# Six of a tile's 32 threshold-search passes counted on ScalarE, the final scaling on GpSimd, and the last search spread over 20 slots

## The chip, the cores and the metric

The kernel runs on one core of a Trainium2 chip. The metric is device time in microseconds (us) of one launch. Engines are called TensorE (PE in the views, PEld for its weight loads), VectorE (DVE), ScalarE (ACT), GpSimd (POOL) and SyncE (SP, which issues the loads and stores).

## The reference, cut to what matters

One inference step of a hybrid attention layer over 2048 prompt positions and 32 sample positions. The change is in the attention over the prompt. There are 8 dense heads (group A) and 8 sparse heads (group B); for B an indexer scores each pair of query and key, and each query keeps its 256 best admissible keys:

```python
rel = jax.nn.relu(jnp.einsum('bqhd,bsd->bqhs', iqb, ik).astype(jnp.float32))
score = jnp.einsum('bqh,bqhs->bqs', iwb.astype(jnp.float32) * w_scale, rel)
adm = (qp[:, None] // CHUNK) >= k_chunk[None, :]
score = jnp.where(adm[None], score, -jnp.inf)
top_val, top_idx = lax.top_k(score, topk)      # topk = 256
...
s = jnp.einsum('bqjgd,bqnjd->bqjgn', qg, kg).astype(jnp.float32) * (dh ** -0.5)
s = jnp.where(valid[:, :, None, None, :], s, -jnp.inf)
p = jax.nn.softmax(s, axis=-1).astype(v.dtype)
o = jnp.einsum('bqjgn,bqnjd->bqjgd', p, vg)
```

Around it stand the input projections before, and the output projection, a gated feed-forward layer and the norms behind.

## The kernel before

The program runs in stages with a barrier between them; `attend_prompt` is the one that changes. It takes the queries in 16 tiles of 128 (n = 0 to 15); tile n sees W = 128(n+1) keys. A tile is 16 **slots**, one for each head (h = 0 to 7 are group A, 8 to 15 group B). Each engine has its own list of instructions written out slot by slot, and semaphores that count events join them.

In slot s (tile n, head h) the engines do this:

- TensorE (block from L1843 on): the scores of the *next* head, in chunks of up to 1024 keys into the two buffers `p_s` (`product`, one chunk for W up to 1024, else two); the value products of the last head's last units; then it turns this head's probabilities over by transposes in units of 512 keys (`turn`), and for tiles with more than two units (n from 8 on) it does this in two pairs of units. Between them stand the products of the indexer for tile n+2 (`index_unit`), in slots 2 to 14.
- ScalarE: a small copy of the last head's sums (`take_halves`), the copies of the turned units out of PSUM (`take`, L1970), the ReLU of the index products (`relu`, L1977), the second pair's copies, and last the exponentials of the next head (`exps`, L1961), which wait for all of that head's minima.
- VectorE: the minimum over each chunk of the next head's scores with the mask added (`minimum`, L2098; the scaled scores go to `prob`), and then its share of the **search** for the tile n+1.
- GpSimd: for each index unit a multiply (L2049) and an add (L2055) into `score`.

The search (`search`, L2105 on) finds each query's 256th best score bit by bit: one pass for the sign and 31 passes for bits 30 to 0. A pass compares all W scores with a candidate and counts (L2118), and two instructions on one column (L2119, L2121) set the next candidate; each waits for the one before (`step`). Five more wide steps (`choose`) make the mask `chosen`, which group B's minima read. `share_by_size` deals these 37 items by an estimated size over 16 slots, from slot 2 of tile m-1 to slot 1 of tile m. The sums of a group of 8 heads are inverted and the output of 128x512 multiplied with them on VectorE in `normed` (L2159 to L2168), in slots 1 and 9.

## Time and profile before

| | us |
|---|---|
| median of 3 runs | 4330.38 (4324.39 to 4334.98) |
| the profiled execution | 4336.22 |
| its span | 4334.2 |
| busy in it: PE, DVE, ACT, POOL | 3780.9, 2278.0, 1687.5, 1350.3 |
| mean granted TensorE clock | 0.935 of full |

Shares over the whole span say little here, since the stages have different limits. The prompt attention runs from about 736 us to 2280.7 us. The stores of its outputs give the borders of its tiles: the second store of tile n-1 is issued in slot 1 of tile n, and from one such store to the next is what is called "tile n" below.

How rows are read: in the windows view a row is one stretch, from:to and its length, then the busy time with the number of instructions of PE, PEld, DVE, ACT and POOL, the granted clock of TensorE as a share of full speed, the share of DMA engines busy and GB/s. In the grouped view a row has line, engine, operation, output<-input, shape and count, then busy us, mean ns of one, and the idle time before the group's instructions. In the view in order of time a row has start, duration, engine, line, operation and shape; a bracket gives idle time just before it and what ended it. READ_ACCUMULATOR rows are the reading out of a sum.

### The profile page before, as it was taken

How to read it: one execution, taken by the hardware profiler on the slowest of the kernel's cores; microseconds unless marked ns; L12 is line 12 of the kernel's file. 1: busy time of each engine (PE TensorE's matmuls, PEld its weight loads, DVE VectorE, ACT ScalarE, POOL GpSimd, SP SyncE). 2: the span in 40 equal slices, each digit the busy share in tenths (PEclk: the TensorE clock that was granted, in tenths of full speed). 3: DMA queues.
4: the chain of work that ended last, by engine and by line, in shares of the span. 5: the costliest groups of instructions: out<-in, count | busy, mean ns of one | idle time of the engine just before them, and what ended most of it. 6: DMA issues, size and time to landing. Idle time of an engine off the chain costs nothing. (4 is left out here: it accounts for less than half of the span.)

```text
span 4334.2 us, 59271 instructions
## 1 busy us (share of the span) xinstructions
PE 3780.9 (87%) x20612; PEld 2891.5 (67%) x20612; DVE 2278.0 (53%) x4226; ACT 1687.5 (39%) x3163; POOL 1350.3 (31%) x845
## 2 busy tenths in 40 slices
PE   7999977878878888888894689699999999999998
PEld 5777743556555555565562567588878778879986
DVE  3222223799999999999943433244044224404421
ACT  3333323555556666665461222232133223213321
POOL 0000001555555556554001000134444444433332
PEclk9999988788999999999896599899999999999999
DMA  4222222110100000000001055533343433433331
GB/s 166 72 83 85 72 68 57 40 32 25 29 22 19 19 17 10 19 17 11 12 6 47 3 189 182 179 97 115 127 116 93 145 121 91 131 111 116 87 101 60
DMA packets 347844, 324.13 MB, mean 75 GB/s; under 512 B 53088, under 2 KB 285120, under 8 KB 347648
## 3 DMA queue, kind: packets, MB, share of 16 engines
q1 hardware_dynamic: 335520, 277.64, 21.9%
q10 hardware_dynamic: 7344, 26.74, 1.5%
q0 software_dynamic: 4800, 17.43, 1.0%
q8 instruction: 102, 1.67, 0.2%
q14 instruction: 78, 0.64, 0.0%
HBM read 251.57 MB, written 71.43 MB: 75 GB/s over the span
## 5 line engine op out<-in xcount | busy, mean ns | idle before, releaser
L1494 POOL TENSOR_TENSOR ff_w_lo<-ff_stage,ff_w_hi 128x2048 fp32r<-128x2048 f32 (+1 forms) x136 | 609.6, 4482 | 1212.3 <-ACT ff_w_hi L1576 1212.3
L2118 DVE TENSOR_SCALAR_CACHE_REDUCE at_hit<-at_score,at_su 128x384 bf16<-128x384 f32 (+13 forms) x434 | 641.2, 1477 | 8.6
L95 PE MATMUL ff_bank<-ff_h_hi,ff_w_hi 128*128 128x512 f32 (+1 forms) x1760 | 618.4, 351 | 30.2 <-DMA ff_h_lo<-scr_h2T 26.5
L96 PE MATMUL ff_bank<-ff_h_lo,ff_w_hi 128*128 128x512 f32 (+1 forms) x1760 | 620.1, 352 | 0.0
L97 PE MATMUL ff_bank<-ff_h_hi,ff_w_lo 128*128 128x512 f32 (+1 forms) x1760 | 618.6, 351 | 0.0
L1638 DVE TENSOR_TENSOR ff_a_lo<-ff_prod,ff_a_hi 128x512 f32 (+1 forms) x110 | 410.4, 3731 | 170.7 <-ACT ff_a_hi L1590 170.7
L1886 PE MATMUL at_p_t<-at_ident,at_prob 128*128 128x128 f32 x2176 | 346.4, 297 | 100.5 <-ACT at_prob L1961 99.0
L1576 ACT ACTIVATE ff_w_hi<-ff_stage 128x2048 fp32r<-128x2048 f32 (+1 forms) x136 | 252.9, 1860 | 443.5 <-PE ff_bank L97 416.2
L1970 ACT ACTIVATE at_probt<-at_p_t 128x512 f32<-128x512 f32 (+3 forms) x640 | 314.9, 532 | 256.3 <-PE at_p_t L1886 254.3
L1961 ACT ACTIVATE at_prob<-at_prob,at_st 128x1024 f32<-128x1024 f32 (+7 forms) x384 | 342.5, 894 | 171.1 <-DVE at_st L2098 170.7
L95 PEld LDWEIGHTS ff_bank<-ff_h_hi,ff_w_hi 128*128 128x128 f32 x1760 | 331.0, 188 | 79.9 <-issue 31.8
L2049 POOL TENSOR_TENSOR at_rel<-at_rel,at_iws 128x512 f32<-128x512 f32 (+3 forms) x304 | 285.6, 939 | 306.3 <-ACT at_rel L1977 305.8
L1886 PEld LDWEIGHTS at_p_t<-at_ident,at_prob 128*128 128x128 f32 x2176 | 249.3, 148 | 183.6 <-ACT at_prob L1961 142.8
L96 PEld LDWEIGHTS ff_bank<-ff_h_lo,ff_w_hi 128*128 128x128 f32 x1760 | 330.8, 188 | 47.2
L97 PEld LDWEIGHTS ff_bank<-ff_h_hi,ff_w_lo 128*128 128x128 f32 x1760 | 330.7, 188 | 46.4
L1873 PE MATMUL at_p_s<-kv_KA,at_qa 96*128 96x512 f32 (+3 forms) x640 | 299.6, 586 | 46.5 <-DVE at_st L2098 40.1
L2055 POOL TENSOR_TENSOR at_score<-at_rel,at_score 128x512 f32<-128x512 f32 (+3 forms) x266 | 305.0, 1147 | 20.8
L1586 ACT ACTIVATE ff_prod<-ff_bank 128x512 f32<-128x512 f32 (+1 forms) x110 | 57.0, 518 | 642.1 <-PE ff_bank L97 642.0
L95 PE MATMUL ff_bank<-ff_w_hi,ff_a_hi 128*128 128x512 f32 (+1 forms) x748 | 295.4, 395 | 3.4 <-POOL ff_w_lo L1494 3.4
L97 PE MATMUL ff_bank<-ff_w_hi,ff_a_lo 128*128 128x512 f32 (+1 forms) x748 | 294.1, 393 | 0.0
L96 PE MATMUL ff_bank<-ff_w_lo,ff_a_hi 128*128 128x512 f32 (+1 forms) x748 | 293.1, 392 | 0.0
L1652 DVE TENSOR_TENSOR ff_x<-ff_bank,ff_x 128x512 f32<-128x512 f32 (+1 forms) x34 | 23.2, 691 | 472.1 <-PE ff_bank L97 472.0
(256 smaller groups left out, 6549.3 us busy)
## 6 DMA issues: line engine op xcount, KB each, us to landing
ff_stage<-in_w_gate SPq DMA_DIRECT2D x88, 512.0 KB, 4.0
ff_stage<-in_w_up SPq DMA_DIRECT2D x88, 512.0 KB, 5.2
ff_stage<-in_w_down SPq DMA_DIRECT2D x40, 1024.0 KB, 5.1
pj_xt<-in_xT SPq DMA_DIRECT2D x17, 512.0 KB, 3.3
pj_x<-in_x SPq DMA_DIRECT2D x17, 512.0 KB, 4.4
scr_qT<-pj_qt SPq DMA_DIRECT2D x68, 128.0 KB, 2.3
mx_o<-scr_o SPq DMA_DIRECT2D x17, 512.0 KB, 7.2
mx_x<-in_x SPq DMA_DIRECT2D x17, 512.0 KB, 3.4
```

Of the source, the lines that this page charges most:

```text
L95: pe.matmul(out, lhs[0], rhs[0], start=start, stop=False)
L96: pe.matmul(out, lhs[0], rhs[1], start=False, stop=False)
L97: return pe.matmul(out, lhs[1], rhs[0], start=False, stop=stop)
L1494: pool.tensor_tensor(w_lo[a][:, 0:w], stage[a][:, 0:w], w_hi[a][:, 0:w].bitcast(F32), ALU.subtract).then_inc(s_wlo, 1)
L1638: dve.tensor_tensor(a_lo[:, ds(2 * q + a, 1), to], prod[b][:, 0:gr.Nh].unsqueeze(1), a_hi[:, ds(2 * q + a, 1), to].bitcast(F32), ALU.subtr ...
L1873: mm = pe.matmul(to, qa[:, h, :], kv["KA"][:, h, a:a + w], start=True, stop=True)
L1886: mm = pe.transpose(p_t[t_turn.at(n, f) % 2][:, b * P:(b + 1) * P], prob[h % 2][:, a + b * P:a + (b + 1) * P], ident[:, :])
L1961: act.activation(to, to, ACT.Exp, bias=negm[:, h:h + 1], scale=-1.0, accum_out=rsum2[:, c, h:h + 1]).then_inc(t_exp.sem, 1)
L1970: act.activation(probt[a][:, 0:w, :], p_t[a][:, 0:w * P], ACT.Copy).then_inc(t_pt.sem, 1)
L2049: pool.tensor_tensor(r, r, iws[:, h:h + 1].broadcast_to([P, w]), ALU.mult).then_inc(t_wtd.sem, 1)
L2055: pool.tensor_tensor(to, r, base, ALU.add).then_inc(t_acc.sem, 1)
L2118: step(dve.tensor_scalar(h_, s_, cand.bitcast(F32), 0.0, ALU.is_ge, ALU.add, cnt))
```

## The change

- In slots 3 to 8 of tile n, one pass of the search for tile n+1 (positions 1 to 6, `HELPED`) is counted by ScalarE: VectorE prepares a threshold in one small instruction and signals (`ask`), ScalarE computes the sign of the scores' upper 16 bits minus it and sums (`sum_signs`), and VectorE waits for the sum before it sets the next candidate (`told`). ScalarE's pass stands behind the copies of the first pair of units.
- The sign pass of each search gets five more instructions on one column.
- For tiles with two chunks, VectorE does the first half of a slot's search items between the two minima; before, both minima came first.
- The search for tile 15 is spread over 20 slots (up to slot 5 of tile 15), that of the others over 16 as before.
- The multiply of `normed` goes to GpSimd, where it waits for ScalarE's copy and for VectorE's reciprocal (`inverse`), which comes at the end of VectorE's slots 1 and 9.
- In tiles 0 to 2 and 15, ScalarE does the next head's exponentials earlier in the slot.
- `tail` (the mask) is bfloat16; it is filled by a copy on GpSimd.

```diff
+        self.span = HA + HB if n < TP - 1 else HA + HB + 4
...
+    HELPED = range(1, 7)
...
-        tail = m.sb("tail", [P, TAIL])
+        tail = m.sb("tail", [P, TAIL], BF16)
...
+        t_ask, t_told = (tally(x, lambda t: len(HELPED) if t.searched else 0) for x in ("candidate_set", "signs_summed"))
+        t_inv = tally("sums_inverted", lambda t: 2)
...
+        def helped(s):
+
+            for k, p in enumerate(HELPED):
+                n = (s - p - SEARCH_FROM) // H + 1
+                if (s - p - SEARCH_FROM) % H == 0 and n < TP and tiles[n].searched:
+                    return n, k
+            return None
...
+                if n and h % HA == 0:
+                    t_norm.wait(act, n - 1, h // HA + 1)
...
+            def sum_signs(n, k):
+                W = tiles[n].W
+                t_ask.wait(act, n, k + 1)
+                top = score[n % 2].bitcast(mybir.dt.int16)[:, 1:2 * W:2]
+                act.activation(signs[:, 0:W], top, ACT.Sign, bias=shift, scale=back, accum_out=signed).then_inc(t_told.sem, 1)
...
+                early = nxt and (n < 3 or n == TP - 1)
                 if s:
                     take_halves(*slots[s - 1])
+                if early and t.U < 3:
+                    exps(*nxt)
...
                 for u in t.pairs[0]:
                     take(n, h, u)
+                if helped(s):
+                    sum_signs(*helped(s))
...
+                if early and t.U > 2:
+                    exps(*nxt)
...
+                if nxt and not early:
                     exps(*nxt)
...
+            def normed(n, g):
+                t_oev.wait(pool, n, g + 1)
+                t_inv.wait(pool, n, g + 1)
+                o = out[:, :].rearrange("p (h d) -> p h d", h=HA)
+                pool.tensor_tensor(o, o, rinv.unsqueeze(2).broadcast_to([P, HA, VA]), ALU.mult).then_inc(t_norm.sem, 1)
...
+                if s > HA and h % HA == 1:
+                    normed((s - 2) // H, (s - 2) % H // HA)
...
-            def minimum(n, h):
+            def minimum(n, h, c):
...
+                    step(dve.tensor_scalar(twice, cnt, TOPK - 0.5, 2.0, ALU.is_lt, ALU.mult))
+                    step(dve.tensor_scalar(flip, twice, -1.0, None, ALU.add))
+                    step(dve.tensor_scalar(back, twice, -1.0, 1.0, ALU.mult, ALU.add))
+                    step(dve.tensor_scalar(least, cnt, twice, None, ALU.mult))
+                    step(dve.tensor_scalar(least, least, -1.0, 2.0 * TOPK - t.W - 0.5, ALU.mult, ALU.add))
...
+                def ask():
+                    step(dve.tensor_scalar(shift, cand_top, flip, 0.5, ALU.mult, ALU.add))
+                    dve.sem_inc(t_ask.sem, 1)
+
+                def told(b, k):
+                    assert b >= 16
+                    t_told.wait(dve, t.n, k + 1)
+                    step(dve.tensor_scalar(miss, signed, least, float(1 << b), ALU.is_lt, ALU.mult))
+                    advance(b)
+
+                size, bits, rest = 1.06 * t.W + 650, list(range(30, -1, -1)), choose(t)
+                total = 1500 + size * (1 + len(bits) - len(HELPED)) + 800 * len(HELPED) + sum(x for x, _ in rest)
+                plan, spent = [], 0
+                for p in range(t.span):
+                    mine = []
+                    if p == 0:
+                        mine, spent = [sign], size + 1500
+                    if p in HELPED:
+                        b = bits.pop(0)
+                        mine.append(lambda b=b, k=HELPED.index(p): told(b, k))
+                        spent += 800
+                    while bits or rest:
+                        cost = size if bits else rest[0][0]
+                        if (spent + cost / 2) * t.span >= total * (p + 1) and p < t.span - 1:
+                            break
+                        spent += cost
+                        if bits:
+                            b = bits.pop(0)
+                            mine.append(lambda b=b: bit(b))
+                        else:
+                            mine.append(rest.pop(0)[1])
+                    if p + 1 in HELPED:
+                        mine.append(ask)
+                    plan.append(mine)
+                return plan
...
-            def normed(n, g):
-                t_oev.wait(dve, n, g + 1)
+            def inverse(n, g):
+                t_exp.wait(dve, n, (g + 1) * HA * tiles[n].C)
                 if 2 * n + g:
                     t_norm.wait(dve, n, g)
                 at = slice(g * HA, (g + 1) * HA)
-                sums, o = rsum2[:, 0, at], out[:, :].rearrange("p (h d) -> p h d", h=HA)
                 if tiles[n].C > 1:
-                    step(dve.tensor_tensor(sums, sums, rsum2[:, 1, at], ALU.add))
-                step(dve.reciprocal(rinv, sums))
-                dve.tensor_tensor(o, o, rinv.unsqueeze(2).broadcast_to([P, HA, VA]), ALU.mult).then_inc(t_norm.sem, 1)
-
+                    step(dve.tensor_tensor(rsum2[:, 0, at], rsum2[:, 0, at], rsum2[:, 1, at], ALU.add))
+                dve.reciprocal(rinv, rsum2[:, 0, at]).then_inc(t_inv.sem, 1)
...
+                todo = [x for m_ in (n, n + 1) if m_ in plans and 0 <= s - (m_ - 1) * H - SEARCH_FROM < tiles[m_].span
+                        for x in plans[m_][s - (m_ - 1) * H - SEARCH_FROM]]
                 if nxt:
-                    minimum(*nxt)
+                    minimum(*nxt, 0)
+                if nxt and tiles[nxt[0]].C > 1:
+                    for do in todo[:(len(todo) + 1) // 2]:
+                        do()
+                    minimum(*nxt, 1)
+                    todo = todo[(len(todo) + 1) // 2:]
+                for do in todo:
+                    do()
                 if s > HA and h % HA == 1:
-                    normed((s - 2) // H, (s - 2) % H // HA)
-                for m_ in (n, n + 1):
-                    t = tiles[m_] if m_ < TP else None
-                    if t and t.searched:
-                        for todo in share_by_size(search(t) + choose(t), s - (m_ - 1) * H - SEARCH_FROM, H):
-                            todo()
-            normed(TP - 1, 1)
+                    inverse((s - 2) // H, (s - 2) % H // HA)
```

VectorE in tile 13, before: slot 3's three passes of the search for tile 14, and the two minima of slot 4 (at_hit with at_score is a pass, ISA with at_prob a minimum, ISA with at_st alone the reading out of it):

```order
L2118 TENSOR_SCALAR at_hit,at_st<-at_score,at_su 128x1920
L2119 TENSOR_SCALAR at_su<-at_st 128x1
L2121 TENSOR_SCALAR at_su<-at_su 128x1
L2118 TENSOR_SCALAR at_hit,at_st<-at_score,at_su 128x1920
L2119 TENSOR_SCALAR at_su<-at_st 128x1
L2121 TENSOR_SCALAR at_su<-at_su 128x1
L2118 TENSOR_SCALAR at_hit,at_st<-at_score,at_su 128x1920
L2119 TENSOR_SCALAR at_su<-at_st 128x1
L2121 TENSOR_SCALAR at_su<-at_su 128x1
L2098 ISA at_prob,at_st<-at_p_s,at_tail 128x1024
L2098 ISA at_st 128x1
L2098 ISA at_prob,at_st<-at_p_s,at_tail,at_st 128x768
```

The same engine now: slot 3 of tile 13 from its first minimum on, and the first minimum of slot 4. L2180 is the candidate step that waits for ScalarE, L2169 a whole pass, L2174 the threshold that ScalarE waits for:

```order
L2138 ISA at_prob,at_st<-at_p_s,at_tail 128x1024
L2138 ISA at_st 128x1
L2180 TENSOR_SCALAR at_su<-at_st 128x1
L2164 TENSOR_SCALAR at_su<-at_su 128x1
L2169 TENSOR_SCALAR at_hit,at_st<-at_score,at_su 128x1920
L2170 TENSOR_SCALAR at_su<-at_st 128x1
L2164 TENSOR_SCALAR at_su<-at_su 128x1
L2138 ISA at_prob,at_st<-at_p_s,at_tail,at_st 128x768
L2138 ISA at_st 128x1
L2174 TENSOR_SCALAR at_st<-at_su,at_st 128x1
L2138 ISA at_prob,at_st<-at_p_s,at_tail 128x1024
L2138 ISA at_st 128x1
```

Three passes used to stand behind both minima. Now the step that waits for ScalarE and one pass stand between the two minima, and in this slot only the threshold stands behind the second; in slots 4, 5 and 6 a second whole pass stands there, ahead of the threshold.

ScalarE in tile 13, before, from the exponentials at the end of slot 2 to those at the end of slot 3 (at_halves and at_probt are copies, at_rel the ReLU):

```order
L1961 ACTIVATE at_prob,at_st<-at_prob,at_st 128x1024
L1961 ACTIVATE at_prob,at_st<-at_prob,at_st 128x768
L1991 ACTIVATE at_halves<-at_p_o 128x128
L1970 ACTIVATE at_probt<-at_p_t 128x512 x2
L1977 ACTIVATE at_rel<-at_p_i 128x512
L1970 ACTIVATE at_probt<-at_p_t 128x512
L1970 ACTIVATE at_probt<-at_p_t 128x256
L1977 ACTIVATE at_rel<-at_p_i 128x512
L1961 ACTIVATE at_prob,at_st<-at_prob,at_st 128x1024
```

And now, where at_signs is the pass of the search:

```order
L1977 ACTIVATE at_prob,at_st<-at_prob,at_st 128x1024
L1977 ACTIVATE at_prob,at_st<-at_prob,at_st 128x768
L2013 ACTIVATE at_halves<-at_p_o 128x128
L1992 ACTIVATE at_probt<-at_p_t 128x512 x2
L1984 ACTIVATE at_signs,at_st<-at_score,at_st 128x1920
L1999 ACTIVATE at_rel<-at_p_i 128x512
L1992 ACTIVATE at_probt<-at_p_t 128x512
L1992 ACTIVATE at_probt<-at_p_t 128x256
L1999 ACTIVATE at_rel<-at_p_i 128x512
L1977 ACTIVATE at_prob,at_st<-at_prob,at_st 128x1024
```

The pass of 1920 scores stands behind the first pair's copies and ahead of the ReLU, the second pair's copies and the next exponentials.

GpSimd in tile 12, around slot 9, before (at_rel and at_score are the index units):

```order
L2055 TENSOR_TENSOR at_score<-at_rel,at_score 128x384
L2049 TENSOR_TENSOR at_rel<-at_rel,at_iws 128x512
L2055 TENSOR_TENSOR at_score<-at_rel,at_score 128x512
L2049 TENSOR_TENSOR at_rel<-at_rel,at_iws 128x512
L2055 TENSOR_TENSOR at_score<-at_rel,at_score 128x512
L2049 TENSOR_TENSOR at_rel<-at_rel,at_iws 128x512
```

And now, with the output's multiply:

```order
L2084 TENSOR_TENSOR at_score<-at_rel,at_score 128x384
L2078 TENSOR_TENSOR at_rel<-at_rel,at_iws 128x512
L2084 TENSOR_TENSOR at_score<-at_rel,at_score 128x512
L2090 TENSOR_TENSOR at_out<-at_out,at_st 128x512
L2078 TENSOR_TENSOR at_rel<-at_rel,at_iws 128x512
L2084 TENSOR_TENSOR at_score<-at_rel,at_score 128x512
L2078 TENSOR_TENSOR at_rel<-at_rel,at_iws 128x512
```

The multiply stands ahead of the slot's first index unit.

## Rows read from the trace of the kernel before

**Rows 1.** Windows view: tiles 6, 8, 13, 14 and 15, and all 16.

```profile
1105.12:1192.90 87.78, 70.53 (x486) 49.63 (x486) 82.39 (x174) 50.66 (x109) 49.05 (x51) 0.94 0.08 23
...
1288.58:1393.91 105.33, 92.50 (x614) 61.35 (x612) 98.13 (x208) 67.68 (x157) 56.56 (x51) 0.94 0.07 20
...
1894.17:2036.78 142.61, 121.50 (x912) 83.12 (x912) 136.37 (x209) 88.38 (x182) 75.85 (x65) 1.00 0.04 11
2036.78:2182.46 145.68, 121.94 (x888) 85.29 (x886) 138.69 (x208) 74.15 (x148) 2.38 (x1) 0.92 0.03 11
2182.46:2280.70 98.24, 92.94 (x820) 68.36 (x816) 39.30 (x62) 64.74 (x130) 2.38 (x1) 1.00 0.02 7
sum 1516.67, PE 1278.95 PEld 881.61 DVE 1348.01 ACT 902.06 POOL 691.36; mean PE 79.93 PEld 55.10 DVE 84.25 ACT 56.38 POOL 43.21
```

**Rows 2.** The grouped instructions of 780 to 2300 us, VectorE.

```profile
L2118 DVE TENSOR_SCALAR_CACHE_REDUCE at_hit<-at_score,at_su 128x384 bf16<-128x384 f32 (+13 forms) x434 | 641.2, 1477 | 8.6
...
L2121 DVE TENSOR_SCALAR at_su<-at_su 128x1 uint32<-128x1 uint32 x420 | 90.0, 214 | 14.9
...
L2119 DVE TENSOR_SCALAR at_su<-at_st 128x1 uint32<-128x1 f32 x434 | 66.8, 154 | 15.1
...
L2118 DVE DVE_READ_ACCUMULATOR at_hit<-at_score,at_su 128x1 f32 x434 | 36.0, 83 | 0.0
L2168 DVE TENSOR_TENSOR at_out<-at_out,at_st 128x512 f32<-128x512 f32 x31 | 35.3, 1139 | 1.1
```

**Rows 3.** VectorE in order of time, tile 13.

```profile
1909.91 1.23 DVE L2098 CUSTOM_DVE_ANT_0 at_prob<-at_p_s,at_tail 128x1024 f32<-128x1024 f32 x1
...
1911.29 1.02 DVE L2098 CUSTOM_DVE_ANT_0 at_prob<-at_p_s,at_tail,at_st 128x768 f32<-128x768 f32 x1
...
1914.92 2.21 DVE L2118 TENSOR_SCALAR_CACHE_REDUCE at_hit<-at_score,at_su 128x1920 bf16<-128x1920 f32 x1
...
1917.18 0.15 DVE L2119 TENSOR_SCALAR at_su<-at_st 128x1 uint32<-128x1 f32 x1
...
1917.62 2.21 DVE L2118 TENSOR_SCALAR_CACHE_REDUCE at_hit<-at_score,at_su 128x1920 bf16<-128x1920 f32 x1
```

**Rows 4.** ScalarE in order of time, the same slot of tile 13.

```profile
1912.35 1.15 ACT L1961 ACTIVATE at_prob<-at_prob,at_st 128x1024 f32<-128x1024 f32 x1 [0.16 <-DVE at_st L2098]
...
1913.50 0.93 ACT L1961 ACTIVATE at_prob<-at_prob,at_st 128x768 f32<-128x768 f32 x1
...
1914.42 0.25 ACT L1991 ACTIVATE at_halves<-at_p_o 128x128 f32<-128x128 f32 x1
1914.62 1.08 ACT L1970 ACTIVATE at_probt<-at_p_t 128x512 f32<-128x512 f32 x2
```

**Rows 5.** TensorE in order of time, a slot of tile 13 with two passes.

```profile
1921.59 1.98 PE L1873 MATMUL at_p_s<-kv_KA,at_qa 96*128 96x512 f32 x4 [1.11 <-DVE at_st L2098]
...
1929.30 1.98 PE L1873 MATMUL at_p_s<-kv_KA,at_qa 96*128 96x512 f32 x4
```

**Rows 6.** The line of the final scaling: shortest, median and longest.

```profile
L2168 DVE TENSOR_TENSOR at_out<-at_out,at_st x32: 691/838/2678, 762.9 to 2279.7; 128x512 f32<-128x512 f32 x32
```

**Rows 7.** GpSimd in order of time, one unit of the index scores.

```profile
1905.52 1.04 POOL L2049 TENSOR_TENSOR at_rel<-at_rel,at_iws 128x512 f32<-128x512 f32 x1
1906.64 1.27 POOL L2055 TENSOR_TENSOR at_score<-at_rel,at_tail 128x512 f32<-128x512 f32 x1
```

**Rows 8.** VectorE in order of time, a slot of tile 6.

```profile
1128.67 1.09 DVE L2098 CUSTOM_DVE_ANT_0 at_prob<-at_p_s,at_tail 128x896 f32<-128x896 f32 x1 [0.33 <-PE at_p_s L1873]
...
1133.74 1.09 DVE L2098 CUSTOM_DVE_ANT_0 at_prob<-at_p_s,at_tail 128x896 f32<-128x896 f32 x1 [0.57 <-PE at_p_s L1873]
```

**Rows 9.** TensorE in the same slot of tile 6.

```profile
1131.34 0.50 PE L1857 MATMUL at_p_i<-kv_KB,at_qi_hi 128*128 128x512 f32 x1 [0.73 <-ACT at_rel L1977]
```

**Rows 10.** VectorE in order of time, tile 15.

```profile
2205.64 1.23 DVE L2098 CUSTOM_DVE_ANT_0 at_prob<-at_p_s,at_tail 128x1024 f32<-128x1024 f32 x1 [2.58 <-PE at_p_s L1873]
...
2213.17 1.23 DVE L2098 CUSTOM_DVE_ANT_0 at_prob<-at_p_s,at_tail 128x1024 f32<-128x1024 f32 x1 [2.58 <-PE at_p_s L1873]
```

More of the change, by code:

```diff
@@ L1767, in attend_prompt @@
         p_t = [m.ps(f"p_t{a}") for a in range(2)]
-        half, negm, rsum, rinv = st[:, 0:2], st[:, 4:20], st[:, 20:52], st[:, 52:60]
+        half, negm, rsum = st[:, 0:2], st[:, 4:20], st[:, 20:52]
+        back, twice, flip, least, shift, signed = (st[:, a:a + 1] for a in range(52, 58))
+        rinv = st[:, 64:72]
         rsum2 = rsum.rearrange("p (e h) -> p e h", e=2)
@@ L2077, in step @@
                 dve.wait_ge(s_vec, done[0])
-            def minimum(n, h):
+            def minimum(n, h, c):
                 t = tiles[n]
                 s = n * H + h
-                if s >= 2:
+                if s >= 2 and c == 0:
                     n2, h2 = slots[s - 2]
```

55 lines of the change are left out of this document (30 added, 25 removed).

## The prediction

> **What bounds the kernel now.** The change touches one stage, so the windows over its tiles come first. There VectorE is the busy engine: 136.4 of 142.6 us in tile 13, 98.1 of 105.3 in tile 8, 82.4 of 87.8 in tile 6, with TensorE at 70.5 to 121.5 and ScalarE and GpSimd far below [rows 1]. What is missing to the full window is mostly the pauses of about 0.04 us between dependent steps. Tile 15, which searches for nobody, is TensorE's: VectorE is busy 39.3 of 98.2 us [rows 1] and idles 2.58 us ahead of a first minimum, one slot being 7.53 us long [rows 10]. The grouped view names VectorE's work: 434 whole passes of the search (14 tiles with 31), at 1.477 us and 0.083 us for reading the sum, most of which lies under the pass's end, then 0.154 and 0.214 us for the candidate [rows 2]. In order of time, from one pass to the next are 2.70 us in tile 13, of which 2.26 us end where the first small step starts [rows 3]. So a slot there is 2.32 us of minima [rows 3] and two or three passes: 7.7 or 10.4 us. In the slots with two, TensorE is full too: 7.71 us from one head's products to the next's, with no idle time [rows 5]. That is the second limit: what VectorE saves in a slot with little work is not all time.
>
> **Off VectorE.** 6 passes in each of 14 searches are 84. Each loses the pass and the reading, 1.477 + 0.083 - 0.08 + 0.04 = 1.52 us on average [rows 2]: -128 us. The multiply of the scaling goes, 35.3 us [rows 2] and its pauses: -36.
> **On VectorE.** Each of the 84 gets a threshold step, about 0.154 + 0.04 us like its neighbour [rows 2], and a signal, taken as 0.05 us: +20. Each sign pass gets five such steps, 14 x 5 x 0.19: +13. Together -131 us. If VectorE bound everywhere and nothing waited, that would be the gain.
>
> **The added wait.** No row shows a sign pass on ScalarE. The nearest are the exponentials: 1.15 us for 1024 columns, 0.93 us for 768 [rows 4], so 0.27 us and 0.86 ns a column; 1920 columns take 1.9 us, 2.0 with the reading of the sum. I take that; below I bound it by half (16-bit input), above by VectorE's 1.04 ns a column, 2.3 us.
> The pass's length is not what decides, but what it is queued behind. In slot s ScalarE must first have done the exponentials of head s, its small copy and the first pair's copies. In tiles 8 to 14 the exponentials now wait for a second minimum that stands in the middle of VectorE's slot. In tile 13, from the end of that minimum: 2.07 us of exponentials (1912.35 to 1914.42), 1.2 us for the copies [rows 4], 2.0 us for the sign pass, 5.3 in all. VectorE meanwhile does the threshold (0.24) and the next first minimum (1.38 us to the next instruction [rows 3]): it waits 3.7 us. Where a whole pass of 2.70 us stands behind the second minimum as well, it waits 1.0. The order has the short form ahead of three of tile 13's six asks: 3 x 3.7 + 3 x 1.0 = 14 us. Tile 14 has four short and two long, with 2.2 us exponentials and a 2.1 us pass: 4 x 4.0 + 2 x 1.2 = 18. Narrower second chunks and passes give 9 in tile 12 and 6.4 to 7.3 in tiles 8 to 11: 27.
> In tiles 1 to 7 there is one chunk, and the exponentials start early as before; the wait is then a pass against a minimum, some 0.3 us, plus what ScalarE is late. In tile 6 the slot of 5.07 us [rows 8] already has TensorE waiting 0.73 us for a ReLU [rows 9], and the sign pass goes in ahead of that ReLU: one wait of 2.6 us and five of 0.8. I take 7 for tile 6, 4 for tile 7, 14 for tiles 1 to 5. Sum of the waits: 14 + 18 + 9 + 27 + 25 = +93. From below 40 (84 x 0.5, ScalarE always free at the ask), from above 125 (ScalarE 0.4 us later in each).
> The Trainium skill, ScalarE: Activation LUTs, section on what ACT_TABLE_LOAD costs, says that each operand that is one value per partition adds about 93 ns to an activation. The exponentials have one such operand, the sign pass has two. No row shows the difference; by it the sum would be 84 x 0.09 = 8 us longer.
>
> **Slots where TensorE is next.** A slot with one helped and one whole pass has 6.7 us of VectorE work after a short wait in tile 13, against TensorE's 7.71 [rows 5]; such slots give back about 1 us, some twelve times: +12 (0 to 22).
>
> **The last search.** Over 20 slots, five of its 25 whole passes go from tile 14 to tile 15: 5 x 2.83 us = -14 (2.70 plus 128 columns at 1.04 ns). In tile 15 two passes and the minima are 8.3 us against 7.53 [rows 10], twice, while slot 0 loses three wide steps: 0 within 3.
>
> **The scaling on GpSimd.** There it takes about 1.27 us [rows 7], and stands ahead of slot 9's index units and waits for VectorE's end of that slot. Two ReLU buffers hold ScalarE free for two units; then the ReLU of slot 10 waits. I take 0.75 us in each of 12 tiles, +9, between 0 and one unit (1.04 + 1.27 [rows 7]) each, 28. Queued behind it are only index adds and, through the ReLU, ScalarE's next exponentials. The Trainium skill, SBUF — State Buffer, holds that VectorE and GpSimd exclude each other on a shared port pair when VectorE reads two SBUF inputs. The rows agree: the multiply took 691 ns at best and 2678 at worst [rows 6]; on GpSimd it can meet VectorE's mask steps in the same way, which no row here prices.
> **The rest.** The earlier exponentials in four tiles: -2 (-8 to +3). Minima apart from each other: they can hide waits of the second for its products, but tile 13 shows none: 0 to -8, taken with the floor above. Narrow mask and changed start: under 1 us.
>
> **Sum.** -131 + 93 + 12 - 14 + 9 - 2 = -33. From the profiled execution's own 4336.2 us that is 4303. That execution lies 5.8 us above the median of the runs, 4330.4; against the median it is 4297.
>
> **Rivals.**
> *ScalarE keeps up.* If TensorE's and ScalarE's slack lets the two chains drift so that the candidate's sum is mostly there, waits fall to 40: 53 us less, 4245. For it: ScalarE is busy only 88 of 142.6 us in tile 13 [rows 1]. Against: its order is fixed, and the copies cannot come before the second minimum.
> *TensorE takes over.* VectorE's load is level now, and every slot could end on TensorE: it is full at 7.71 us in tile 13 [rows 5], so that outside of tile 14 nothing is left, and only the 14 us there: 4316, or 4325 with GpSimd's term. Against: TensorE idles over 1 us in the slots with three passes [rows 5].
> *Slower: the sign pass is in TensorE's loop.* In tiles 1 to 7 the loop copies, sign pass, ReLU, index product, next head's products closes in every helped slot, as the 0.73 us wait begins to show [rows 9]. A mean pass of 1216 columns is 1.4 us; 42 such slots are +59 us, and the result is 4330 - 33 + 59 = 4356. It decides as soon as that loop is longer than VectorE's slot, which in tile 6 is 5.07 us [rows 8] and becomes less.
> *A table load for Sign.* The Trainium skill, ScalarE: Activation LUTs, has functions in sets and a load at each change of set; 84 passes with two loads would cost far over 100 us. The program's order has one load at the stage's start, before and after, so I give this no chance of its own.
>
> **How the numbers follow.** Forecast 0.50, ScalarE keeps up 0.20, TensorE takes over 0.15, slower 0.15. A difference of 0.3% (13 us) is about what can be told from none. The forecast's own range is 4275 to 4325; nine tenths of it are faster by more. Faster: 0.45 + 0.20 + 0.01 = 0.66; same: 0.05 + 0.12 = 0.17; slower: 0.15 + 0.02 = 0.17. The range takes in most of the first rival and ends inside the last: 4255 to 4335.
>
> **What would show it.** VectorE's busy time in the stage falls by about 130 us, and there are 84 waits of VectorE for the sign pass, about 90 us in all, near 4 us in tiles 13 and 14 where the threshold stands directly behind the second minimum and near 1 us elsewhere. Sign passes of 1920 columns take about 2.0 us. Tile 14 shortens by 8 to 16 us, tiles 8 to 13 by 0 to 4 each, tile 15 hardly moves. The forecast is wrong if waits in tiles 13 and 14 are under 2 us (the first rival), if tiles 3 to 7 are longer than before (the slower one), or if VectorE idles for products in most slots (TensorE takes over).

## The result, and the profile of the changed kernel

The changed kernel took 4368.4 us (median of 4 runs, 4365.9 to 4374.0), the kernel before 4327.4 beside it: a ratio of 1.0107, 95% interval 1.0085 to 1.0129. It is 41 us slower; the forecast was 33 faster, and its range ended at 4335. Times in this text are medians of a kernel's runs; one execution of c2 below took 9756.9 us instead of about 4278 and is left out of them. The profiled execution took 4365.9 us for itself, 29.7 more than that of before. Its page begins with the busy time of each engine:

```profile
PE 3765.4 (86%) x20612; PEld 2892.6 (66%) x20612; DVE 2136.7 (49%) x4180; ACT 1787.8 (41%) x3331; POOL 1376.8 (32%) x878
```

VectorE has lost 141 us of work, 10 more than forecast. So the work left, and the time did not. The windows view shows where. Its columns are the stretch, its length, the busy time and count of PE, PEld, DVE, ACT and POOL, the granted clock of TensorE, DMA share and GB/s. These are tiles 1, 2, 7, 8, 13, 14 and 15 of the changed kernel, of which tiles 8 and 13 to 15 answer to [rows 1]:

```profile
778.79:836.99 58.20, 43.35 (x179) 28.55 (x177) 40.35 (x163) 28.13 (x87) 25.36 (x21) 0.59 0.12 35
836.99:906.50 69.51, 48.50 (x255) 31.41 (x255) 48.95 (x169) 36.65 (x99) 31.80 (x38) 0.78 0.10 29
1210.26:1314.08 103.82, 79.60 (x530) 54.18 (x528) 79.28 (x177) 62.12 (x126) 53.92 (x53) 0.90 0.07 20
1314.08:1420.13 106.05, 86.60 (x621) 59.48 (x619) 87.78 (x205) 74.21 (x169) 57.83 (x53) 0.98 0.07 20
1917.74:2062.45 144.71, 126.63 (x898) 89.47 (x897) 118.67 (x205) 97.70 (x190) 77.34 (x67) 0.93 0.04 11
2062.45:2199.95 137.50, 115.91 (x887) 83.48 (x886) 106.96 (x188) 86.00 (x159) 4.45 (x3) 0.94 0.04 12
2199.95:2313.06 113.11, 94.50 (x803) 68.02 (x801) 49.67 (x71) 65.64 (x126) 4.44 (x3) 0.98 0.02 6
```

In tile 13 VectorE is busy 118.7 of 144.7 us where it had been busy 136.4 of 142.6 [rows 1]: 26 us of idle time stand where 6 stood. The tiles' lengths, read in the same way, show where the time went:

| tiles | before, us | changed, us | difference |
|---|---|---|---|
| 1 and 2 | 107.3 | 127.7 | +20.4 |
| 3 to 7 | 396.0 | 407.5 | +11.5 |
| 8 to 13 | 748.2 | 748.4 | +0.2 |
| 14 | 145.7 | 137.5 | -8.2 |
| 15 | 98.2 | 113.1 | +14.9 |

Together +38.8 us; tile 0 ends 6.6 us earlier than before, and the rest of the program is 2 us shorter. That gives the 29.7 us between the two profiled executions; the one of before was 9 us over its median and the other 2 under, and so the medians lie 41 apart.

TensorE's granted clock is lower in tiles 1 (0.59, before 0.75) and 13 (0.93, before 1.00), and this is not what made them long: in b1 below, tile 1 took 48.5 us at 0.64 and tile 13 took 143.4 at 0.95, within 1 us of before.

What the idle time ends with is in the waits view of the changed kernel, 780 to 2350 us (who waited, for whom, total us, times, longest):

```profile
POOL at_out L2090 <- DVE at_st L2247: 333.1, 29, 67.9
...
ACT at_prob L1977 <- DVE at_st L2138: 146.6, 89, 3.7
DVE at_su L2180 <- ACT at_signs L1984: 145.4, 77, 4.4
...
DVE at_prob L2138 <- PE at_p_s L1872: 68.8, 42, 4.4
...
ACT at_rel L1999 <- POOL at_score L2084: 53.7, 25, 4.7
...
PE at_p_o L1920 <- ACT at_probt L1992: 39.4, 30, 3.2
```

The third row is the added wait: 145 us, forecast 93. GpSimd's 333 us in the first cost nothing by themselves: it waits for VectorE's reciprocal before a block that has slack, except where the fifth row follows from it. The last row hardly existed before (1.4 us in 4 waits).

The grouped view of VectorE answers to [rows 2] (after the bar: busy us, mean ns, then idle before it and its releaser):

```profile
L2169 DVE TENSOR_SCALAR_CACHE_REDUCE at_hit<-at_score,at_su 128x384 bf16<-128x384 f32 (+13 forms) x350 | 517.0, 1477 | 5.7
...
L2180 DVE TENSOR_SCALAR at_su<-at_st 128x1 uint32<-128x1 f32 x84 | 18.0, 214 | 146.2 <-ACT at_signs L1984 145.4
L2174 DVE TENSOR_SCALAR at_st<-at_su,at_st 128x1 f32<-128x1 int16 x83 | 17.7, 213 | 2.3
```

84 passes are gone, at the same mean of 1.477 us. The same 84 stand on ScalarE; this is their line in the changed kernel (min/median/max ns, first and last start):

```profile
L1984 ACT ACTIVATE at_signs<-at_score,at_st x84: 695/1396/2114, 779.9 to 2123.4; 128x384 uint8<-128x384 int16 x6, 128x512 uint8<-128x512 int16 x6, 128x640 uint8<-128x640 int16 x6, 128x768 uint8<-128x768 int16 x6
```

Now the same place as [rows 3]: VectorE in order of time, tile 13 of the changed kernel (start us, length us, ..., idle before and releaser in brackets).

```profile
1930.46 0.21 DVE L2180 TENSOR_SCALAR at_su<-at_st 128x1 uint32<-128x1 f32 x1 [3.71 <-ACT at_signs L1984]
...
1930.96 2.21 DVE L2169 TENSOR_SCALAR_CACHE_REDUCE at_hit<-at_score,at_su 128x1920 bf16<-128x1920 f32 x1
...
1933.65 1.02 DVE L2138 CUSTOM_DVE_ANT_0 at_prob<-at_p_s,at_tail,at_st 128x768 f32<-128x768 f32 x1
...
1934.60 0.21 DVE L2174 TENSOR_SCALAR at_st<-at_su,at_st 128x1 f32<-128x1 int16 x1
1935.06 1.22 DVE L2138 CUSTOM_DVE_ANT_0 at_prob<-at_p_s,at_tail 128x1024 f32<-128x1024 f32 x1 [0.25 <-DVE at_st L2174]
...
1940.61 0.21 DVE L2180 TENSOR_SCALAR at_su<-at_st 128x1 uint32<-128x1 f32 x1 [4.32 <-ACT at_signs L1984]
```

The second minimum (1933.65), at once the threshold (1934.60), the next first minimum (1935.06), then nothing for 4.3 us: the short form of the ask, forecast at 3.7. ScalarE over the following slot answers to [rows 4]:

```profile
1944.86 1.15 ACT L1977 ACTIVATE at_prob<-at_prob,at_st 128x1024 f32<-128x1024 f32 x1
...
1946.01 0.92 ACT L1977 ACTIVATE at_prob<-at_prob,at_st 128x768 f32<-128x768 f32 x1
...
1946.93 0.25 ACT L2013 ACTIVATE at_halves<-at_p_o 128x128 f32<-128x128 f32 x1
1947.36 1.09 ACT L1992 ACTIVATE at_probt<-at_p_t 128x512 f32<-128x512 f32 x2 [0.18 <-PE at_p_t L1900]
1948.33 1.99 ACT L1984 ACTIVATE at_signs<-at_score,at_st 128x1920 uint8<-128x1920 int16 x1
```

Exponentials, small copy, first copies, and only then the sign pass, at 1.99 us (forecast 2.0). From the first exponential to the end of the pass are 5.5 us, of which the pass is 2.0: the queue ahead of it costs more than the pass.

Tile 15 tells the part that was not foreseen. ScalarE in order of time, changed kernel, second head group:

```profile
2270.23 1.15 ACT L1977 ACTIVATE at_prob<-at_prob,at_st 128x1024 f32<-128x1024 f32 x1 [1.60 <-DVE at_st L2138]
...
2271.38 1.13 ACT L1977 ACTIVATE at_prob<-at_prob,at_st 128x1024 f32<-128x1024 f32 x1
...
2272.51 1.05 ACT L1992 ACTIVATE at_probt<-at_p_t 128x512 f32<-128x512 f32 x2
...
2277.59 1.15 ACT L1977 ACTIVATE at_prob<-at_prob,at_st 128x1024 f32<-128x1024 f32 x1 [1.60 <-DVE at_st L2138]
```

TensorE at the same place:

```profile
2271.45 0.40 PE L1872 MATMUL at_p_s<-kv_KB,at_qb_lo 128*128 128x512 f32 x1
2273.14 1.14 PE L1920 MATMUL at_p_o<-at_probt,kv_VB 128*64 128x128 f32 x16 [1.30 <-ACT at_probt L1992]
```

and VectorE's second minimum of that head:

```profile
2268.91 1.28 DVE L2138 CUSTOM_DVE_ANT_0 at_prob<-at_p_s,at_chosen,at_st 128x1024 f32<-128x1024 f32 x1 [3.04 <-PE at_p_s L1872]
```

The early exponentials stand ahead of the copies of the second pair. ScalarE idles 1.60 us for the second minimum, then does 2.3 us of exponentials, and only then the copies, for which TensorE idles 1.30 us. But that second minimum itself has waited 3.04 us for TensorE's products. The loop is closed, once a head, and a head of this group takes 7.36 us (2270.23 to 2277.59). In the kernel before, the same exponentials stand behind the copies and start without a pause, 5.94 us apart:

```profile
2245.80 1.15 ACT L1961 ACTIVATE at_prob<-at_prob,at_st 128x1024 f32<-128x1024 f32 x1
...
2251.74 1.15 ACT L1961 ACTIVATE at_prob<-at_prob,at_st 128x1024 f32<-128x1024 f32 x1
```

Eight heads at 1.4 us more would be 11 of the tile's 15 us, by estimate from these rows. VectorE's first minima in the first head group of the changed kernel answer to [rows 10]:

```profile
2206.60 1.22 DVE L2138 CUSTOM_DVE_ANT_0 at_prob<-at_p_s,at_tail 128x1024 f32<-128x1024 f32 x1
2214.68 1.23 DVE L2138 CUSTOM_DVE_ANT_0 at_prob<-at_p_s,at_tail 128x1024 f32<-128x1024 f32 x1 [1.32 <-PE at_p_s L1887]
2222.91 1.23 DVE L2138 CUSTOM_DVE_ANT_0 at_prob<-at_p_s,at_tail 128x1024 f32<-128x1024 f32 x1 [1.32 <-PE at_p_s L1887]
```

These two slots take 8.1 and 8.2 us, against 7.53 [rows 10].

Last, the scaling on GpSimd, which answers to [rows 6]: 1.042 us each time, where VectorE took 0.69 to 2.68.

```profile
L2090 POOL TENSOR_TENSOR at_out<-at_out,at_st x32: 1041/1042/1047, 762.1 to 2311.7; 128x512 f32<-128x512 f32 x32
```

### The profile page after: what moved, and what is told of

Read it like the earlier page. It is cut to its first block and busy times, and to the rows that moved or that the text cites. A ratio compares the mean times of both kernels' runs of the same rounds, so it can differ in the third digit from the quotient of the medians.

```text
span 4364.1 us, 59572 instructions
## 1 busy us (share of the span) xinstructions
PE 3765.4 (86%) x20612; PEld 2892.6 (66%) x20612; DVE 2136.7 (49%) x4180; ACT 1787.8 (41%) x3331; POOL 1376.8 (32%) x878
## 5 line engine op out<-in xcount | busy, mean ns | idle before, releaser
L2169 DVE TENSOR_SCALAR_CACHE_REDUCE at_hit<-at_score,at_su 128x384 bf16<-128x384 f32 (+13 forms) x350 | 517.0, 1477 | 5.7
L1887 PE MATMUL at_p_s<-kv_KA,at_qa 96*128 96x512 f32 (+3 forms) x640 | 286.6, 564 | 6.8 <-DMA at_prob<-in_causal_bias 6.1
```

Of the source, the lines that this page charges most:

```text
L1887: mm = pe.matmul(to, qa[:, h, :], kv["KA"][:, h, a:a + w], start=True, stop=True)
L2169: step(dve.tensor_scalar(h_, s_, cand.bitcast(F32), 0.0, ALU.is_ge, ALU.add, cnt))
```

## The experiments

Ratios are to the kernel before, run on the same chip at the same time, with 95% intervals; "us" are differences of these ratios times 4325. Names that begin with e are edits of the changed kernel, those with b and c2 are edits of the kernel before, and c1 and c3 are edits of e6 and e8. Lengths of tiles and waits are of each kernel's one profiled execution.

**Four parts taken back one at a time.** The early exponentials:

```diff
-                early = nxt and (n < 3 or n == TP - 1)
+                early = False
```

> The changed kernel with the next head's exponentials at the end of ScalarE's slot in every tile, as before (early = False). Theory A, early exponentials are most of the loss: in tiles 1 and 2 they put the copies behind a minimum that VectorE reaches only after its ask, and in tile 15 the second pair's copies behind a minimum of which TensorE's products come late. Tiles 1 and 2 lose 20 us and tile 15 loses 15 us of the 41; without them the time is 4368 - 35 = 4333, tile 15 back at about 98 us, tiles 1 and 2 at 47 to 50 and 57 to 61. Rival B, tile 15 is long because of the search spread into it and the split minima, and tiles 1 and 2 because of the added waits for ScalarE: the time stays within 10 us of 4368.

Measured: 4331.1 us, 1.0022 (1.0004 to 1.0039), 37 us less than the changed kernel. Tiles 1 and 2 lose 21.6 us, tile 15 loses 16.6 (113.1 to 96.5).

```diff
-    HELPED = range(1, 7)
+    HELPED = range(0)
```

> The changed kernel with no pass on ScalarE (HELPED empty; VectorE does all 31, the five small steps in the sign pass stay). Theory A, the early exponentials are the loss wherever they stand: tile 15 stays at 113 us, and the 145 us of waits of VectorE for the sign passes go against 84 passes of 1.52 us less 84 threshold steps, +110: 4368 - 35 = 4333, with tiles 1 and 2 short again since the copies' lateness then holds nobody. Rival C, the helped passes pay on balance and the loss is elsewhere: the time rises to 4390 or more.

Measured: 4305.0 us, 0.9963 (0.9944 to 0.9981), 62 us less. No theory had it so large: the passes on ScalarE, which were the aim of the change, cost time in this arrangement. Tile 15 stays at 111.6 us, so the early exponentials cost there without any sign pass; tiles 1 and 2 come back to 108.2, so there they cost only together with it.

```diff
                 if nxt and tiles[nxt[0]].C > 1:
-                    for do in todo[:(len(todo) + 1) // 2]:
-                        do()
                     minimum(*nxt, 1)
-                    todo = todo[(len(todo) + 1) // 2:]
```

> The changed kernel with both minima of a head ahead of the search's items, as before. Theory D, in tiles 8 to 14 VectorE's waits (90 us in those seven tiles) are long because the exponentials wait for a minimum in the middle of the slot: together they start some 3 us sooner, waits fall to about 1 us, 45 us in all, and tile 15's TensorE waits change little: 4368 - 35 = 4333, less up to 15 us that TensorE's own slots give back, so 4333 to 4348. Rival E, the order of the minima is neutral as ScalarE is then held by the ask itself and TensorE's next products by the same minima: within 10 us of 4368.

Measured: 4319.6 us, 0.9995 (0.9979 to 1.0011), 48 us less, more than either theory gave. VectorE in order of time, tile 13 of this kernel:

```profile
1921.01 1.23 DVE L2138 CUSTOM_DVE_ANT_0 at_prob<-at_p_s,at_tail 128x1024 f32<-128x1024 f32 x1 [0.25 <-DVE at_st L2174]
...
1923.10 1.02 DVE L2138 CUSTOM_DVE_ANT_0 at_prob<-at_p_s,at_tail,at_st 128x768 f32<-128x768 f32 x1 [0.86 <-PE at_p_s L1887]
...
1924.45 0.21 DVE L2180 TENSOR_SCALAR at_su<-at_st 128x1 uint32<-128x1 f32 x1 [0.33 <-ACT at_signs L1984]
```

and the waits view of the stage:

```profile
DVE at_su L2180 <- ACT at_signs L1984: 68.2, 51, 3.9
```

With the second minimum right behind the first, the exponentials are out of the way a whole pass earlier, and the sign pass is done by the time it is wanted. In tiles 8 to 14 the waits fall from 90 us to 14; what is left stands in tiles 1 to 7. In the profiled executions tiles 1 to 15 together get 41 us shorter, 37 of them in tiles 8 to 14 (885.9 to 848.7); another 10 us lie behind the attention, where the edit changes nothing. So the edit itself is worth 41 to 48 us.

The multiply of the scaling back on VectorE, in `inverse`, and the calls of `normed` on GpSimd taken out (not shown):

```diff
-                dve.reciprocal(rinv, rsum2[:, 0, at]).then_inc(t_inv.sem, 1)
+                step(dve.reciprocal(rinv, rsum2[:, 0, at]))
+                o = out[:, :].rearrange("p (h d) -> p h d", h=HA)
+                dve.tensor_tensor(o, o, rinv.unsqueeze(2).broadcast_to([P, HA, VA]), ALU.mult).then_inc(t_norm.sem, 1)
```

> The changed kernel with the output's multiply back on VectorE, in its slots 1 and 9 behind the search's items. Theory F, GpSimd's block in slot 9 (ScalarE waited 54 us for it in 25 places) costs about what VectorE's 36 us of multiplies cost: within 12 us of 4368. Rival G, the block is a main part of the loss: 4340 or less. Rival H, the block is hidden and VectorE's time counts in full: 4395 or more.

Measured: 4376.6 us, 1.0133 (1.0101 to 1.0165), 11 us more (the intervals overlap). ScalarE's waits for GpSimd's adds fall from 53.7 us to 1.2 with it, and still it is no faster: the move was no part of the loss. But it gains little here, 11 us within the noise of the two, against 27 forecast.

**Are the parts independent?** e5 takes e1 and e3 together; e6 takes the helped passes out as well.

> Both at once: exponentials late in every tile, and both minima ahead of the search's items. Theory A+D: the two losses lie in different tiles (1, 2 and 15 against 8 to 14) and add up. After against each: -37 and -49 us, so 4368 - 86 = 4282. Rival: they share the late second minimum, in tile 15 above all, and the sum is smaller: 4300 to 4320.

> The same with no pass on ScalarE: what is left of the change is the scaling on GpSimd, the last search over 20 slots, the five small steps in each sign pass, the narrow mask. Theory I, with the minima together the helped passes pay: VectorE has 84 x (1.52 - 0.24) = 107 us more work, against 68 us of waits in the run with minima together less those of tiles 1 and 2 (21): the time is 4282 + 30 to 60, 4310 to 4340. Rival J, ScalarE's passes cost TensorE and ScalarE more than VectorE saves even so, in the tiles up to 7 above all: 4282 or less.

Measured: e5 4288.2 us, 0.9922 (0.9902 to 0.9941); e6 4303.2 us, 0.9948 (0.9929 to 0.9967). The two edits add up (80 us against 37 + 48), and with them the helped passes turn from a loss of 62 us to a gain of about 11 to 15. That gain is two parts: from e6 to e5, tiles 8 to 14 get 33 us shorter with help (881.0 to 848.3) and tiles 1 to 7 get 22 us longer (491.2 to 512.9). e6 against e2 shows the other side: without helped passes, e6 should win the 17 us of the early exponentials in tile 15, and it is only 2 to 6 better. That leaves some 11 us that minima apart from each other may be worth where no sign pass depends on them. Tiles 11 to 13 fit it (126.8, 133.8 and 139.0 us in e2, 131.4, 137.7 and 144.9 in e6), but no run makes this edit alone in a kernel without helped passes.

**Where do they pay?** e7 is e5 with help only in the searches of tiles 9 to 15, that is while tiles 8 to 14 run; the five small steps are gone from the other seven searches as well, so that it makes two edits. e8 is e7 with GpSimd's scaling a slot later, behind the index adds.

```diff
+    HELP_FROM = 9
-        t_ask, t_told = (tally(x, lambda t: len(HELPED) if t.searched else 0) for x in ("candidate_set", "signs_summed"))
+        t_ask, t_told = (tally(x, lambda t: len(HELPED) if t.n >= HELP_FROM else 0) for x in ("candidate_set", "signs_summed"))
+                    if t.n < HELP_FROM:
+                        return
...
+                HELPED = range(1, 7) if t.n >= HELP_FROM else range(0)
```

> As the first of these, with helped passes only in the searches for tiles 9 to 15, done in tiles 8 to 14 with two pairs of units; the five small steps too only there. Theory K, in tiles 1 to 7 the sign pass stands in TensorE's loop between the copies and the ReLU and pays nothing: tiles 6 and 7 go from 96 and 100 us to about 86 and 93, the others lose 0 to 2 us, in all 15 to 20 us under the first of these. Rival: the passes level the load there too, and the time is that of the first within 5 us or longer.

```diff
-                if s > HA and h % HA == 1:
-                    normed((s - 2) // H, (s - 2) % H // HA)
                 for part in range(2):
                     for q in index_units(s, part):
                         add(n + 2, q)
+                if s > HA and h % HA == 2:
+                    normed((s - 3) // H, (s - 3) % H // HA)
```

> As the one before, with GpSimd's multiply of the output one slot later, behind the index units of slots 2 and 10. Theory L, the 58 us in which ScalarE waits for GpSimd's adds come from the block in slot 9, where GpSimd waits for the end of VectorE's slot; one slot later the reciprocal is there and the waits vanish, of which TensorE and VectorE feel a part: 8 to 20 us less. Rival: VectorE's slots hide the block, and the time stays within 5 us.

Measured: e7 4257.6 us, 0.9852 (0.9828 to 0.9876), 30 us less than e5. Tiles 3 to 7 fall from 404.3 us to 378.6. The two edits in it can be told apart by e6, which has no help but has the small steps, and by c1 below, which has neither: tiles 3 to 7 take 386.6 and 377.9 us. So 18 of the 26 us are the sign passes, and 8 to 9 are the small steps. The waits view of tile 6 shows what the sign passes do; in e5 (1101.88 to 1196.12 us):

```profile
PE at_p_i L1871 <- ACT at_rel L1999: 18.8, 11, 5.0
DVE at_su L2180 <- ACT at_signs L1984: 10.3, 4, 3.6
```

and in e7 (1092.86 to 1176.46 us):

```profile
PE at_p_i L1872 <- ACT at_rel L2000: 11.8, 11, 4.3
```

TensorE's waits for a ReLU are 18.8 us with sign passes in the queue ahead of the ReLU and 11.8 without. They were 8.3 us in 11 before the change, the longest 0.8 us, so some 3 us come without any sign pass. e8: 4249.1 us, 0.9824 (0.9803 to 0.9845), 12 us less by the ratios, 9 by the medians, intervals overlapping; ScalarE's waits for GpSimd's adds fall from 67.3 to 3.6 us, as its theory said.

**Parts put alone into the kernel before.** The last search over 20 slots (`t.span` for `H` in `share_by_size`), the early exponentials, and the scaling on GpSimd:

> The kernel before with one part of the change: the search for tile 15 over 20 slots. The prediction's term: five whole passes leave tile 14, -14 us, and tile 15 takes them beside TensorE, 0 within 3: 4324 - 14 = 4310. Rival: tile 15's first slots give the time back, as TensorE is full there (7.53 us a slot against 8.3): 4318 to 4326.

> The kernel before with one part of the change: the exponentials of the next head early in ScalarE's slot in tiles 0 to 2 and 15. Theory A1: tile 15 loses by itself, 17 us as in the runs with and without it, since the second pair's copies stand behind a minimum that waits for TensorE's products; tiles 1 and 2 lose next to nothing, since their 20 us came from the early exponentials together with the helped passes (without helped passes they were 50.3 and 57.9 us): 4324 + 17 = 4341. Rival A2: in tiles 1 and 2 it costs by itself as well, 20 us more: 4361.

> The kernel before with one part of the change: the output's multiply on GpSimd, in slots 1 and 9, the reciprocal at the end of VectorE's slot. The prediction's terms: -36 on VectorE, +9 for GpSimd's block: 4324 - 27 = 4297. Theory L: the block costs more, some 10 to 20 us, as moving it by a slot gained 8 us with ScalarE's waits going from 67 to 4 us: 4305 to 4315.

Measured: b1 4309.3 us, 0.9956 (0.9933 to 0.9978), 19 by the ratio and 11 by the medians (4320.35 beside it); tile 14 falls from 145.7 to 125.7 us and tile 15 stays (98.8). `share_by_size` moves more here than the plan of the changed kernel: VectorE's busy time in tile 15 grows by 19 us (39.3 to 58.0), in the changed kernel by 10 (to 49.7), so this run bounds the term from above. b2 4339.6, 1.0041 (1.0023 to 1.0059), +18 to +19, nearly all in tile 15 (98.2 to 115.0). TensorE of b2 in tile 15 shows the same wait as the changed kernel:

```profile
2228.36 1.14 PE L1906 MATMUL at_p_o<-at_probt,kv_VA 128*64 128x128 f32 x16 [1.30 <-ACT at_probt L1970]
```

b3 4287.9, 0.9923 (0.9901 to 0.9945), -32 to -33 us.

**Is it what the pass is queued behind?** e1 with the sign pass ahead of the first pair's copies:

```diff
+                if helped(s):
+                    sum_signs(*helped(s))
                 for u in t.pairs[0]:
                     take(n, h, u)
-                if helped(s):
-                    sum_signs(*helped(s))
```

> The changed kernel with late exponentials everywhere, and the sign pass ahead of the first units' copies. Theory M, VectorE's wait is the sum of what stands ahead of the pass: in tiles 8 to 14 (87 us of waits in 42 places) the copies' 1.1 us go in each place where the wait was over 1.1 us, so waits there fall by 35 to 45 us; the copies and with them TensorE's value products come later by a pass of 1.6 to 2.1 us, which in tiles 1 to 7 stands ahead of everything TensorE waits for. Time 4331 - 15 within 15 us. Rival N, the exponentials and the ask set the wait alone: it stays at 87 us within 10, and the time rises by 10 to 30 us for TensorE.

Measured: 4290.9 us, 0.9920 (0.9898 to 0.9942), 40 to 44 us less than e1. The waits of tiles 8 to 14 fall from 87.4 to 50.5 us, those of the stage from 120 to

```profile
DVE at_su L2180 <- ACT at_signs L1984: 68.6, 75, 3.0
```

The pass, its length and VectorE's order are the same; only the first pair's copies have changed places with it. That shows the queue ahead of the pass as the cause of the wait. It has a price: TensorE's waits for the copies grow from 1.4 to 38.2 us, and the kernel is faster all the same.

**Small parts and combinations.** c1 is e6 without the five small steps, c2 is b1 and b3 together, c3 is e8 with the minima apart in the slots without help:

```diff
+                    first = 0 if helped(s) or helped(s + 1) else (len(todo) + 1) // 2
+                    for do in todo[:first]:
+                        do()
                     minimum(*nxt, 1)
+                    todo = todo[first:]
```

> The run with late exponentials, minima together and no helped pass, without the five small steps in each sign pass. Theory O, the steps cost what they last, 14 x 5 x 0.19 = 13 us: 4303 - 13 = 4290. Rival: they are hidden, and it stays at 4303 within 4.

> The kernel before with the scaling on GpSimd and the last search over 20 slots. Theory P, the two gains lie in different places and add up: 4320 - 33 - 11 = 4276 to 4280. Rival Q: they share slots in which TensorE ends next, and the time is that of the run above, 4290 or more.

> The fastest run so far (4249) with the minima apart in those slots that neither have nor precede a helped pass. Theory R, apart they hide VectorE's waits for the second chunk's products where nobody waits for their exponentials: without helped passes the kernel with them apart was 14 us shorter in tiles 11 to 13; 5 to 15 us less, 4235 to 4245. Rival: later exponentials hold TensorE, which is nearly full in these tiles: no change or up to 10 us more.

Measured: c1 4282.8 us, 0.9907 (0.9889 to 0.9926), 18 us less than e6. c2 4277.8, 0.9887 (0.9866 to 0.9907); the gains add. c3 4240.0, 0.9812 (0.9796 to 0.9828); against e8 that is 5 to 9 us with overlapping intervals, inconclusive for the edit. It is the fastest kernel here, 81 to 85 us (1.9%) under before and 128 under the changed one.

## Why the prediction was wrong

**The steps that failed** are the two reorderings in "The rest", both priced at next to nothing. Both taken back (e5), the kernel is 34 us faster than before, where the forecast had 33; that the number is so near is luck, for the terms below are off in both directions.

**The first**: "The earlier exponentials in four tiles: -2 (-8 to +3)". They cost 37 us in the changed kernel (e1), 18 to 19 alone (b2). I looked at when the exponentials may start, not at which of ScalarE's instructions they then stand ahead of. In tile 15 these are copies for which TensorE waits. In tiles 1 and 2 it is the sign pass. ScalarE in order of time, tile 1 of the changed kernel:

```profile
792.61 0.51 ACT L1977 ACTIVATE at_prob<-at_prob,at_st 128x256 f32<-128x256 f32 x1 [3.01 <-DVE at_st L2138]
...
793.38 0.70 ACT L1984 ACTIVATE at_signs<-at_score,at_st 128x384 uint8<-128x384 int16 x1
```

VectorE at the same place:

```profile
792.14 0.42 DVE L2138 CUSTOM_DVE_ANT_0 at_prob<-at_p_s,at_tail 128x256 f32<-128x256 f32 x1 [0.25 <-DVE at_st L2174]
...
794.21 0.21 DVE L2180 TENSOR_SCALAR at_su<-at_st 128x1 uint32<-128x1 f32 x1 [1.63 <-ACT at_signs L1984]
```

The early exponentials need the minimum that VectorE does after the ask. ScalarE idles 3.01 us for it. The ask has ended by 791.89 (the minimum follows it after 0.25 us), but the pass can begin only behind the minimum, the exponentials and the copy, at 793.38. In e1 the same wait of VectorE, in tile 1, is short:

```profile
801.65 0.21 DVE L2180 TENSOR_SCALAR at_su<-at_st 128x1 uint32<-128x1 f32 x1 [0.24 <-ACT at_signs L1984]
```

**The added wait, +93: mechanism right, size off.** It was 145 us, above the upper bound of 125. By tiles, forecast and measured: tile 13, 14 and 15.7; tile 14, 18 and 19.9; tile 12, 9 and 12.5; tiles 8 to 11, 27 and 42; tiles 6 and 7, 11 and 23; tiles 1 to 5, 14 and 32. Those at and next to the rows that they were worked out from, tiles 13 and 14, were good; those scaled down from them were not. Narrower tiles make the passes shorter, but not the copies, the ReLU and the waits for them. About 25 us of the 52 too many belong to the early exponentials (120 us are left in e1).

**The second: the minima apart, "0 to -8".** Behind that line was a gain for TensorE, which is there (about 11 us by e6 against e2, perhaps 5 to 9 by c3, neither shown by itself). But with sign passes the added wait hangs on them: it is this large because the second minimum stands in the middle of the slot. The forecast saw that link ("the exponentials now wait for a second minimum that stands in the middle of VectorE's slot"), and then priced the two edits in two places, so that nothing said 48 us hang on the one. e3 does.

**VectorE's work, -131: right**, -141 on the page. But busy time is not time. The ask was taken as 0.24 us and is 0.46: the step of 0.21 and 0.25 us of idle time ahead of the minimum that follows (1934.60 to 1935.06 above), and so 0.22 us more each time. In the waits view 58 minima idle behind the ask's step, 14.7 us in all, which no busy time shows; elsewhere a later wait covers it. The five small steps cost 18 us (c1), forecast 13.

**The last search, -14: right as far as shown** (b1: -11 to -19, with more work moved), with tile 15 unchanged by it. **Scaling on GpSimd, -36 + 9 = -27: right in the kernel before** (b3: -32 to -33), and only 11 in the changed one, within the noise (e4). Its wait was real and larger, 54 us of ScalarE's waits in place of 9, but most of it under cover: with that wait gone, e8 won 9 to 12.

**Slots where TensorE is next, +12**: not measured by itself. The changed kernel has VectorE waiting for products in 72 places, 104 us in all, against 78 before.

**The rivals.** The slower one, "the sign pass is in TensorE's loop", gave 4356, and it is the one nearest to the time. It is real, but smaller: by e5 against e6 the sign passes cost 22 us in tiles 1 to 7. Its price of 59 was wrong in itself: it took the mean pass of all 14 searches (1216 columns) for slots of tiles 1 to 7, whose passes have 384 to 1152 columns, 768 on average; at the measured 1.0 us for such a pass, 42 slots are 43 us. And it is not the reason why the sum has the wrong sign: with the two reorderings taken back, help in all tiles is a gain (e5 against e6). ScalarE did not keep up (the waits are 145, not 40), though in e3's order it does in tiles 8 to 14, at 14 us in all. TensorE's loop took over in tile 15, by the early exponentials and not by VectorE's relief.

**What would show it** held for VectorE's busy time, the waits near 4 us in the short form (3.7 to 4.4 in tiles 13 and 14) and near 1 us in the long (1.1 to 1.6), the 2.0 us pass and tile 14 (-8.2). It failed for the sum of the waits (145, not about 90), for tiles 8 to 13, of which three are shorter and three longer (-3.0 to +4.5, +0.2 in all), for tile 15 (+14.9, "hardly moves") and for tiles 3 to 7 (+11.5), the last named as the sign of the slower rival.

Of the 74 us between forecast and result, then: early exponentials 39, of which about 25 us are waits; other waits for sign passes 27; the ask 15; small steps 5; less 5 on the scaling. These are 81. They are sizes and not a closed sum: the terms overlap, the 48 us of the minima apart are inside the waits and the rest, VectorE's busy time fell 10 us more than forecast, by e4 the scaling would be 16 us short instead of 5 over, and the floor of +12 may not have been due. How they share the difference stays open.

## What to carry to other kernels

When work moves to an engine with slack, write down that engine's queue in the slot, with the instruction each entry waits for: the result comes when everything ahead of it has been released and done, and an entry that waits for the asking engine's next step (as the early exponentials did) makes a loop that no busy time shows. An edit that only reorders is not free to price at zero; name what it is moved ahead of, and who waits for that. Two edits that touch the same wait (where the second minimum stands, and the pass queued behind it) are priced together or not at all: the helped passes lost 62 us in one order and won 11 to 15 in another.

## What the runs showed of the hardware

The sign pass over every second 16-bit value, with the sum read, takes 695 ns for 384 columns and 2114 for 2048: 0.853 ns a column and 0.37 us besides. So 16-bit input did not halve it, the lower bound of the forecast. The exponentials have 0.27 us besides in [rows 4], so the second operand of one value per partition comes to about 0.1 us. The Trainium skill, ScalarE: Activation LUTs, section on what ACT_TABLE_LOAD costs, has about 93 ns for it, and the trace agrees.

On VectorE the threshold step with its signal left 0.25 us of idle time ahead of the minimum behind it, while dependent small steps follow each other at 0.04. The minimum alone does not make it: in the same trace 148 minima that stand behind a small step without an ask start 0.03 to 0.04 us after it. Whether the signal or the ask's own step does, no run separated.

GpSimd's multiply of 128x512 took 1.042 us within 6 ns over 32 instances, while the same on VectorE spread from 0.69 to 2.68 us [rows 6]. The traces show what each met. Every multiply of VectorE over 0.7 us overlapped an instruction of GpSimd, and where GpSimd's began second, it was the one that took longer (1.36 us instead of 1.04 at 862.02 in the kernel before). GpSimd's multiply in the changed kernel overlapped only minima and passes of VectorE, each with one wide operand in SBUF. The Trainium skill, SBUF — State Buffer, section on who interferes with whom, has the two engines exclude each other where VectorE reads two operands from SBUF, and the traces agree. So what the prediction held possible, that on GpSimd the multiply meets VectorE's mask steps, did not happen in the profiled execution.
